# Modulation pieces of layer 1 moved from the end of layer 0's experts into the heads of a DeltaNet layer

## The chip, the cores and the metric

The kernel runs on one core of a Trainium2 chip. The metric is the device time of one execution in microseconds (us): the median of three runs is 1553.63 us (1552.72 to 1554.36).

## The reference, cut to what matters

One inference step of a two-layer backbone over 128 context tokens and 512 latent tokens of 1024 features (five tiles of 128 tokens). Layer 0 is attention beside a convolution module, layer 1 a bidirectional gated DeltaNet with 8 heads; each layer ends in a mixture of 16 experts. Both layers are modulated by rows that come from a conditioning vector (one for the context, one for the latents):

```python
def modulation(cond, w, b):
    return (jax.nn.silu(cond) @ w + b)[:, None, :]      # w: 1024 x 6144, per layer

for layer in range(DEPTH):
    mod_p = jnp.split(modulation(c_ctx[None], w_mod[layer], b_mod[layer]), MOD_CHUNKS, -1)
    mod_s = jnp.split(modulation(c, w_mod[layer], b_mod[layer]), MOD_CHUNKS, -1)
    hp = modulate(rms_norm(xp, g_norm1[layer]), mod_p[0], mod_p[1])
    hs = modulate(rms_norm(xs, g_norm1[layer]), mod_s[0], mod_s[1])
    ...                                                  # attention (0) or DeltaNet (1)
    xp = xp + mod_p[2] * mp
    xs = xs + mod_s[2] * ms
    xp = xp + mod_p[5] * hier_moe(modulate(rms_norm(xp, g_norm2[layer]), mod_p[3], mod_p[4]), *mo)
    xs = xs + mod_s[5] * hier_moe(modulate(rms_norm(xs, g_norm2[layer]), mod_s[3], mod_s[4]), *mo)
```

The change concerns the last five of the twelve column blocks (512 columns each) of layer 1's modulation. Their rows are first used after the eight heads of the DeltaNet layer, in the gate of its output and in its experts.

## The kernel before, in words

Every engine runs its own hand-written list of instructions; semaphores order them across engines, and nothing is scheduled by a planner. The stages in order are layer 0's projections and attention, its output and routing, its experts (about 424 to 624 us), a norm and the gates of layer 1 (to 660 us), the eight heads (to 1198 us), the output, and layer 1's experts to the end.

**Modulation steps.** A step is half a column block: sixteen products of a 128x2 stationary operand (the two conditioning vectors) with 128x128 pieces of the weights (`block_rows`, line 343; a product shows as two matrix instructions in the trace). There are 40 steps; 30 lie beside earlier work. The last ten (`late_load`, `late_steps`) lie at the end of layer 0's experts: SyncE (SP) loads ten pieces of 1 MB each (line 329) into buffers that the experts have given up, and TensorE (PE) does the products after the last expert tile, five steps before it reports the end of its stage and five after. ScalarE (ACT) copies the sums out of PSUM at the start of the next stage (`comb0_act`, line 1965).

**The end of the experts.** Fourteen tiles of 128 routed tokens are gathered, multiplied and scattered back into `ysum` with an accumulating indirect DMA that GpSimd (POOL) issues (line 1724). A scatter waits for the one before it. After the fourteen tiles comes a loop of at least one extra tile, with its own loads (lines 1651, 1652, 1655), gather and scatter. Layer 1's experts (to the end of the kernel) are the same code with other weights and no modulation steps. When all four engines have reported the end (`comb_sp`), SP loads `ysum` (line 1957) and the norm of layer 1 begins; PE does some products that nobody reads in between (line 1463, `unread_products`).

**A head.** PE builds the inverse of a triangular matrix in `levels` (5120 small 32x32 products over the heads, line 2345), alternating with VectorE (DVE) and `fill` pieces of the next head's projection (line 2283); then it runs a scan of five steps (`keys_on_state` 2415, `solve` 2421, `queries_on_state` 2427, `values` 2432 and 2434), again alternating with DVE (residuals 2701, outputs 2729 and 2731) and ACT, with `fill` pieces in the gaps. In the last step:

```python
values(h, 3)
fill(3)
keys_on_state(h, 4)
fill(3)
solve(h, 4)
fill(3)
queries_on_state(h, 4)
values(h, 4)
fill(5)                      # then levels(h + 1) waits for outputs(h, 4) of DVE
```

SP's list for head h (`heads_sp`) is: decay rows of the next head (line 2069), wait for the last values of the head before, two state loads of 64 KB (2084), the weights of head h+2 in three loads of 512 KB (2064; for the last two heads instead one 2 MB load, 2090), and the stores of two final states (2093). POOL adds the bias to the modulation rows, stores them and loads the gate rows (`finish_rows`, `load_gate_rows`) at the start of its part of the heads (`heads_pool`), ahead of its masks for head 0 (2822 to 2825).

Of the kernel before, what the change touches and what calls it, by code (L numbers as in the profile page):

```python
# [22 lines left out]
P = 128  # L23
# [94 lines left out]
def build_program(nc, I, O):  # L118
    with ExitStack() as ctx:
        def sb(name, shape, dt=F32):  # L120
# [13 lines left out]
                 "cb_y0": ("mod_w0", 16), "cb_y1": ("mod_w1", 16), "cb_y2": ("mod_w2", 16), "cb_y3": ("mod_w3", 16), "cb_y4": ("mod_vec", 64),  # L134
                 "hd_kT": ("mod_vecT", 4), "hd_tkn": ("mod_col_mm", 4), "hd_kk": ("mod_step_mm", 40),
                 "hd_cp": ("mod_vec_ev", 4), "hd_silu": ("cond_ready", 1), "hd_rk": ("in_hT_act", 10), "hd_knT": ("mod_raw", 6),
# [4 lines left out]
                 "hd_rows": ("in0_w_lat", 16), "hd_states": ("in0_w_glu", 32), "mod_late_w0": ("mod_step_w0", 240), "mod_late_w1": ("mod_step_w1", 240)}  # L141

# [17 lines left out]
        ring = sb("ring", [P, 3, 4096])  # L160
# [53 lines left out]
        phase_no = {}  # L214
# [38 lines left out]
        def load_act(act):  # L253
# [19 lines left out]

        late_slot = [ring[:, 1, 0:2048], ring[:, 1, 2048:4096], hbuf_flat[:, 0:2048], at(8192, 2048), at(10240, 2048),
                     ring[:, 2, 2048:4096], modN_flat[:, 0:2048], hT_flat[:, 0:2048], hT_flat[:, 2048:4096], modN_flat[:, 2048:4096]]
        LATE_FIRST = 5
        LATE_FREE = [("gu", 12), ("gu", 12), ("x", 24), ("gu", 13), ("gu", 13), ("dn", 24), ("dn", 26), ("gu", 14), ("gu", 14), ("dn", 28)]

        def step_slot(i):
            if i >= MSTEP_LATE:  # L280
                return late_slot[i - MSTEP_LATE]
            return at(2048 + 2048 * (i % 2), 2048) if i < MSTEP_IN0 else ring[:, 0, 2048 * (i % 2):2048 * (i % 2 + 1)]
# [9 lines left out]
        def step_psum(i):  # L292

            l, b, half = step_block(i)
            n = b - 4
            if b < 4:
                return bank(7, P, b * P)
            if l == 0:
                return bank(7, P, n * P) if n < 4 else bank(3, P, (n - 4) % 4 * P)
            return bank(7, P, n % 3 * P) if n < 3 else bank(7, P, (n - 3) * P) if n < 7 else bank(0, P)  # L300

# [20 lines left out]

        def late_load(sp, i):
            l, b, half = step_block(i)
            j = i - MSTEP_LATE
            what, n = LATE_FREE[j]
            sp.wait_ge(S({"gu": "moe0_gu_mm", "x": "moe0_xT", "dn": "moe0_dn_mm"}[what]), n)
            w = I["w_mod"][l].rearrange("(k p) n -> p k n", p=P)
            sp.dma_start(step_slot(i).rearrange("p (k n) -> p k n", k=4),
                         w[:, 4 * half:4 * half + 4, b * 512:(b + 1) * 512]).then_inc(S(f"mod_late_w{j // LATE_FIRST}"), 16)  # L330

        def late_steps(pe, part):
            count_wait(pe, f"mod_late_w{part}", 16 * LATE_FIRST)
            for i in range(MSTEP_LATE + LATE_FIRST * part, MSTEP_LATE + LATE_FIRST * (part + 1)):
                l, b, half = step_block(i)
                block_rows(pe, step_slot(i), step_psum(i), 4 * half, 4 * half + 4).then_inc(S("mod_step_mm"), 1)

# [1311 lines left out]
        def moe_sp(sp, l):  # L1649
# [55 lines left out]
            with sp.Fori(0, n) as i:  # L1705
# [3 lines left out]
                down_at(e, 0)  # L1709
            if l == 0:  # L1710
                for i in range(MSTEP_LATE, MSTEP):
                    late_load(sp, i)

# [64 lines left out]
        def moe_pe(pe, l):  # L1778
# [77 lines left out]
            with pe.Fori(0, n) as i:  # L1856
# [4 lines left out]
                down(i + NS, 0, part(NS), i * 16 + 80)  # L1861
            if l == 0:
                late_steps(pe, 0)
                arrive(pe, "pe")
                late_steps(pe, 1)
                for other in ("act", "dve", "pool"):
                    pe.wait_ge(S(f"{other}_phase_done"), phase_no["moe0"])
            else:
                barrier(pe, "pe", "moe1")

# [92 lines left out]
        def comb0_act(act):  # L1963
            act.activation(view(small, 1099, 1), C("eps"), ACT.Sqrt)
            raw_out(act, MSTEP, raw_row[:, 3 * P:7 * P], bank(7))
            act.copy(raw_row[:, 7 * P:8 * P], bank(0, P)).then_inc(S("mod_raw"), 1)

            def square(t):
                act.wait_ge(S("cb_used"), t + 1)
                act.activation(junk[:], X[:, t, :], ACT.Square, accum_out=ss[:, t:t + 1])  # L1970
                act.drain()
                act.activation(rstd[:, t:t + 1], ss[:, t:t + 1], ACT.Sqrt, scale=1.0 / D, bias=C("eps")).then_inc(S("norm_rms"), 1)

            for t in range(NT):
# [77 lines left out]
        def heads_sp(sp):  # L2052
# [23 lines left out]
            count_wait(sp, "hd_rows", 16)  # L2076
            decay_rows(0)
            for h in range(H):
                if h + 1 < H:
# [3 lines left out]
                for c, name in ((0, "state_fwd"), (1, "state_bwd")):  # L2083
                    sp.dma_start(St[:, c, :], I[name][0, 0, h]).then_inc(S(f"hd_st{c}"), 16)
                if h + 2 < H:
                    head_weights(h + 2)
# [15 lines left out]
        def gates_pe(pe):  # L2102
# [13 lines left out]
            unread_products(pe, 3)  # L2116
            pe.wait_ge(S("mod_raw"), 6)
            for t in range(NT):
# [152 lines left out]
        def heads_pe(pe):  # L2271
# [172 lines left out]
            for h in range(H):  # L2444
# [24 lines left out]
                values(h, 1)  # L2469
                fill(1)  # L2470
                if more:
                    k_to_tokens(n)
# [16 lines left out]
                fill(1)  # L2489
                queries_on_state(h, 3)  # L2490
                values(h, 3)
                fill(3)
                keys_on_state(h, 4)
                fill(3)
                solve(h, 4)
                fill(3)
                queries_on_state(h, 4)
                values(h, 4)
                fill(5)
            barrier(pe, "pe", "heads1")  # L2500

        def heads_act(act):
# [103 lines left out]
            for h in range(H):  # L2606
# [6 lines left out]
                if more:  # L2613
                    take_unit(n, 0)
                inverse_blocks(h)
                if more:
                    take_unit(n, 1)
# [192 lines left out]
        def heads_pool(pool):  # L2810
            pool.memset(TTp, 0.0)
            pool.drain()
            pool.wait_ge(S("mod_bias"), 320)
            finish_rows(pool, 1, 3, 8)
            pool.wait_ge(S("mod_stored"), 192)
            load_gate_rows(pool, 1, 2, "mod_bc")
            for h in range(H):
# [6 lines left out]
                count_wait(pool, "hd_masked", 2 * h + 1)  # L2824
                pool.tensor_tensor(NTm, A, rep(betam[:, h, :], P, 2), ALU.mult).then_inc(S("hd_masked"), 1)
            barrier(pool, "pool", "heads1")

# [186 lines left out]
```

## Time and profile before

| | |
|---|---|
| median of three runs | 1553.63 us (1552.72 to 1554.36) |
| the profiled execution | 1549.61 us |
| its span, first to last instruction | 1547.5 us |
| mean granted TensorE clock | 0.971 |
| busy share of the span | PE 90%, PE weight load 62%, DVE 53%, ACT 30%, POOL 13% |
| bytes moved by DMA | 265.45 MB, mean 172 GB/s |

The profile is of one execution. A busy share is an average over stages with different limits, so the stages are read one by one: the chain of work that ended last says which engine or transfer set the time of each stretch, and the timelines of the engines say how much another engine had left beside it. In a timeline the columns are the start and the duration of a group of instructions, then the engine, the line, the operation, the tiles written and read, the size and the count; a bracket gives the idle time before the group and what ended it. "issue" there is time in which the engine waited for nothing that the profile shows.

### The profile page before, as it was taken

The page shows a single profiled execution, that of the slowest core. Times are in us where ns is not written, and L with a number is a line of the kernel's source. Part 1 is how long each engine was busy: PE and PEld are TensorE (multiplying, and loading weights), DVE is VectorE, ACT ScalarE, POOL GpSimd, SP SyncE. Part 2 cuts the span into 40 slices and gives each one's busy share as a digit, 9 for nine tenths or more (in the row PEclk, how much of TensorE's full clock was granted, in tenths as well). Part 3 has the DMA queues.
Part 4 walks back from the last instruction along what each step waited for, and adds up shares of the span by engine and source line. Part 5 has one row for each costly group of instructions (what it writes and reads, how often), then busy time and mean ns, then how long its engine had stood idle before and what let it go on. Part 6 is the DMA issues. An engine that isn't in the chain of part 4 may idle for free.

```text
span 1547.5 us, 33618 instructions
## 1 busy us (share of the span) xinstructions
PE 1397.3 (90%) x14422; PEld 964.2 (62%) x14422; DVE 814.2 (53%) x1604; ACT 470.1 (30%) x1057; POOL 205.1 (13%) x199
## 2 busy tenths in 40 slices
PE   4999989999899997779998898998988999899993
PEld 3555557745487776456776776776755445587772
DVE  2377678736633432535666565665653726544331
ACT  3101755512100000544555544554522202100000
POOL 2200020101321212131011010110100001312221
PEclk9999999999999998889999999999999999999997
DMA  9954673222799999521101201111010432899985
GB/s 344 339 168 136 201 236 121 72 109 109 253 369 360 386 368 299 158 90 41 46 22 49 64 23 47 52 37 60 6 61 4 163 127 104 294 367 374 380 288 132
DMA packets 103412, 265.45 MB, mean 172 GB/s; under 512 B 7648, under 2 KB 37608, under 8 KB 93888
## 3 DMA queue, kind: packets, MB, share of 16 engines
q1 hardware_dynamic: 88096, 206.22, 36.7%
q0 software_dynamic: 15168, 57.08, 12.9%
q8 instruction: 114, 1.87, 0.5%
q14 instruction: 34, 0.28, 0.1%
HBM read 235.29 MB, written 35.32 MB: 175 GB/s over the span
## 4 chain that ended last, share of the span: by engine, by line
PE 61%; DMA 13%; DVE 11%; issue 7%; ACT 4%; DVEq 2%; POOL 1%; POOLq 0%; ACTq 0%; SPq 0%
DMA ysum<-arena,small 11%; PE psum L983 8%; PE psum L2283 8%; PE psum L1794 5%; PE psum L635 5%; PE psum L2345 4%; PE psum L1805 3%; PE psum L2295 2%; PE psum L2842 2%; PE psum L343 2%; PE psum L533 2%; PE psum L999 2%; PE psum L1010 1%; PE psum L1022 1%; DVE modN L2655 1%
## 5 line engine op out<-in xcount | busy, mean ns | idle before, releaser
L2283 PE MATMUL psum<-hT,ring 128*128 128x384 f32 (+1 forms) x736 | 242.9, 455 | 0.7 <-ACTq L218 0.7
L2283 PEld LDWEIGHTS psum<-hT,ring 128*128 128x128 f32 x736 | 129.1, 195 | 35.4 <-issue 3.9
L1794 PEld LDWEIGHTS psum<-arena,ring 128*128 128x128 f32 x1024 | 119.0, 196 | 12.3 <-issue 10.3
L1794 PE MATMUL psum<-arena,ring 128*128 128x128 f32 x1024 | 120.5, 280 | 4.1 <-DVE arena L1873 4.1
L1915 DVE TENSOR_TENSOR arena<-arena,psum 128x256 f32<-128x256 f32 x30 | 12.6, 421 | 191.0 <-PE psum L1794 166.5
L792 DVE SCALAR_TENSOR_TENSOR arena<-arena,params_sb 128x655 f32<-128x655 f32 x120 | 106.1, 906 | 6.3 <-issue 0.9
L2345 PEld LDWEIGHTS psum<-arena 32*32 32x32 f32 x5120 | 54.7, 109 | 65.7 <-issue 38.0
L1724 POOL DMA_INDIRECT ysum<-arena,small x34 | 57.6, 1693 | 263.4 <-DMA ysum<-arena,small 138.2
L2345 PE MATMUL psum<-arena 32*32 32x32 f32 x5120 | 63.6, 198 | 30.4 <-issue 18.7
L983 PE MATMUL psum<-ring,arena 128*128 128x512 f32 x160 | 72.6, 608 | 1.0 <-ACTq L218 1.0
L635 PE MATMUL psum<-hT,ring 128*128 128x512 f32 (+1 forms) x256 | 72.1, 438 | 0.7 <-ACT modN L463 0.7
L1894 ACT ACTIVATE arena<-psum 128x256 f32<-128x256 f32 x30 | 11.5, 384 | 200.6 <-PE psum L1794 173.0
L983 PE MATMUL psum<-ring,hT 128*128 128x512 f32 x160 | 70.7, 596 | 1.2 <-ACTq L218 1.2
L1873 ACT COPY arena<-psum 128x512 f32<-128x512 f32 x30 | 17.6, 586 | 167.0 <-PE psum L1786 167.0
L2822 POOL TENSOR_TENSOR arena<-arena,consts_sb 128x640 f32<-128x640 f32 x8 | 10.5, 1317 | 383.7 <-PE psum L2395 383.4
L1805 PE MATMUL psum<-ring,arena 128*128 128x512 f32 x128 | 57.8, 594 | 1.3 <-DVE arena L1915 1.3
L635 PEld LDWEIGHTS psum<-hT,ring 128*128 128x128 f32 x256 | 38.3, 191 | 30.8 <-issue 30.8
L983 PEld LDWEIGHTS psum<-ring,arena 128*128 128x128 f32 x160 | 30.1, 194 | 36.5 <-issue 34.7
L983 PEld LDWEIGHTS psum<-ring,hT 128*128 128x128 f32 x160 | 29.7, 190 | 36.1 <-issue 34.6
L1305 DVE TENSOR_TENSOR arena<-psum,modG 128x512 f32<-128x512 f32 x20 | 13.8, 689 | 69.7 <-PE psum L983 69.7
L1881 DVE SCALAR_TENSOR_TENSOR arena<-psum,small,junk 128x512 f32<-128x512 f32 x60 | 42.8, 748 | 11.0 <-PE psum L1805 7.0
L1794 PEld LDWEIGHTS psum<-arena 128*128 128x128 f32 x384 | 43.8, 192 | 2.9 <-issue 2.9
(517 smaller groups left out, 2753.5 us busy)
## 6 DMA issues: line engine op xcount, KB each, us to landing
arena<-in_w_mod SPq DMA_DIRECT2D x18, 1024.0 KB, 5.3
ring<-in_m_w_gate SPq DMA_DIRECT2D x18, 1024.0 KB, 7.3
ring<-in_m_w_up SPq DMA_DIRECT2D x18, 1024.0 KB, 9.5
ring<-in_m_w_down SPq DMA_DIRECT2D x18, 1024.0 KB, 10.9
ring<-in_w_mod SPq DMA_DIRECT2D x17, 1024.0 KB, 5.5
modN<-in_m_w_down SPq DMA_DIRECT2D x16, 1024.0 KB, 13.4
ring<-in_c_w_in SPq DMA_DIRECT2D x24, 512.0 KB, 6.4
arena<-in_m_w_gate SPq DMA_DIRECT2D x8, 1024.0 KB, 8.4
```

The costliest lines, as they stand in the source:

```text
L343: m = pe.matmul(out[32 * j:32 * j + 2, :], cond[:, k, :], w[:, c0:c0 + P], start=(k == 0), stop=(k == KC - 1))
L533: m = pe.matmul(bank(t, LAT), hT[:, k, tok(t)], ring[:, 0, k * LAT:(k + 1) * LAT], start=(k == 0), stop=(k == KC - 1))
L635: m = pe.matmul(out, ring[:, s, c0:c0 + P], hT[:, k, o:o + n], start=(k == 0), stop=(k == KC - 1))
L792: m = dve.scalar_tensor_tensor(out=acc[:, fc, :], in0=src, scalar=conv_w(fc, k), in1=acc[:, fc, :], op0=ALU.mult, op1=ALU.add)
L983: m = pe.matmul(out_bank(l, n), lhs[:, k, tok(t)], ring[:, OUT_SLOT[l][nb], k * 512:(k + 1) * 512], start=(k == 0), stop=(k == KC - 1))
L999: m = pe.matmul(bank(b, n0), qT[0:QK, h, tok(qt)], kT[0:QK, h, k0 * P:k0 * P + n0], start=True, stop=True)
L1724: pool.indirect_dma_start(out=ysum[l], out_offset=bass.IndirectOffsetOnAxis(ap=idx, axis=0), in_=yb[q][part, :], in_offset=None, compute_o ...
L1794: m = pe.matmul(bank((2, 4)[half] + (1, 3)[half] * q, P, f * P), gu_slot[s][:, c0:c0 + P], xgT[:, q, k, :], start=(k == 0), stop=(k == KC ...
L1805: m = pe.matmul(bank(5 + nb), hidT[:, q, k, :], dn_slot[s][:, k * D + nb * 512:k * D + nb * 512 + 512], start=(k == 0), stop=(k == 1))
L1881: dve.scalar_tensor_tensor(out=yb[q][:, c], in0=bank(5 + half), scalar=w, in1=gate_row[:, c], op0=ALU.mult, op1=ALU.mult).then_inc(S(f"moe ...
L2283: m = pe.matmul(bank(un % 2, w), ring[:, s, c0k:c0k + P], hT[:, k, o:o + w], start=(k == 0), stop=(k == KC - 1))
L2345: m = pe.matmul(bank(b, 32, 32 * i)[QD(q), :], lhs(5 * g + i, q), rhs(5 * g + i, q), start=True, stop=True)
```

## The change

The ten late steps leave the end of layer 0's experts. Each of the first five heads now takes one column block: SP loads its 2 MB in five pieces into free parts of `ring` and `arena`, and PE does its 32 products in four places of the head's last scan step, eight products (sixteen matrix instructions) a place. For head 0 the load follows the first decay rows; for heads 1 to 4 it stands between the state loads and the loads of weights, behind a wait for the last late products of the head before. PE waits for the load and for DVE's transition before the first place. ACT copies the sums out in the next head, between the inverse blocks and a projection copy, and PE waits for that copy ahead of `k_to_tokens`. POOL's finishing of the rows moves from before its masks of head 0 to after those of head 7. The semaphore counts that follow from this are adjusted.

```diff
-        late_slot = [ring[:, 1, 0:2048], ring[:, 1, 2048:4096], hbuf_flat[:, 0:2048], at(8192, 2048), at(10240, 2048),
-                     ring[:, 2, 2048:4096], modN_flat[:, 0:2048], hT_flat[:, 0:2048], hT_flat[:, 2048:4096], modN_flat[:, 2048:4096]]
+        LATE_HEADS = (MSTEP - MSTEP_LATE) // 2
+        late_slot = [ring[:, 0, 3072:4096], ring[:, 1, 3072:4096], at(15360, 1024), ring[:, 2, 640:1152], ring[:, 2, 3200:3712]]
+        late_row = lambda k: late_slot[k // 2][:, k % 2 * 512:k % 2 * 512 + 512] if k < 6 else late_slot[k - 3]
+        LATE_K = [(0, 2), (2, 4), (4, 6), (6, 8)]
...
-        def late_load(sp, i):
...
+        def late_load(sp, h):
+            if h >= 1:
+                count_wait(sp, "late_mm", h)
+            l, b, _ = step_block(MSTEP_LATE + 2 * h)
             w = I["w_mod"][l].rearrange("(k p) n -> p k n", p=P)
+            k = 0
+            for slot in late_slot:
+                n = slot.shape[1] // 512
+                sp.dma_start(slot.rearrange("p (k n) -> p k n", k=n), w[:, k:k + n, b * 512:(b + 1) * 512]).then_inc(S("late_w"), 16)
+                k += n
+
+        def late_rows(pe, h, part):
+            if part == 0:
+                count_wait(pe, "late_w", 16 * len(late_slot) * (h + 1))
+                count_wait(pe, "hd_nt", h + 2)
+            for k in range(*LATE_K[part]):
+                m = block_rows(pe, late_row(k), bank(3, P, 2 * P), k, k + 1)
+            if part == len(LATE_K) - 1:
+                m.then_inc(S("late_mm"), 1)
...
# moe_sp
-            if l == 0:
-                for i in range(MSTEP_LATE, MSTEP):
-                    late_load(sp, i)
# moe_pe
-            if l == 0:
-                late_steps(pe, 0)
-                arrive(pe, "pe")
-                late_steps(pe, 1)
-                for other in ("act", "dve", "pool"):
-                    pe.wait_ge(S(f"{other}_phase_done"), phase_no["moe0"])
-            else:
-                barrier(pe, "pe", "moe1")
+            barrier(pe, "pe", f"moe{l}")
# comb0_act
-            raw_out(act, MSTEP, raw_row[:, 3 * P:7 * P], bank(7))
-            act.copy(raw_row[:, 7 * P:8 * P], bank(0, P)).then_inc(S("mod_raw"), 1)
# heads_sp
             decay_rows(0)
+            late_load(sp, 0)
...
                     sp.dma_start(St[:, c, :], I[name][0, 0, h]).then_inc(S(f"hd_st{c}"), 16)
+                if 1 <= h < LATE_HEADS:
+                    late_load(sp, h)
                 if h + 2 < H:
                     head_weights(h + 2)
# gates_pe
-            pe.wait_ge(S("mod_raw"), 6)
# heads_pe
                 values(h, 1)
                 fill(1)
+                if 1 <= h <= LATE_HEADS:
+                    count_wait(pe, "late_raw", h)
                 if more:
                     k_to_tokens(n)
...
+                late = (lambda part: late_rows(pe, h, part)) if h < LATE_HEADS else (lambda part: None)
                 values(h, 3)
                 fill(3)
+                late(0)
                 keys_on_state(h, 4)
                 fill(3)
+                late(1)
                 solve(h, 4)
                 fill(3)
+                late(2)
                 queries_on_state(h, 4)
                 values(h, 4)
                 fill(5)
+                late(3)
# heads_act
                 inverse_blocks(h)
+                if 1 <= h <= LATE_HEADS:
+                    count_wait(act, "late_mm", h)
+                    act.copy(raw_row[:, (2 + h) * P:(3 + h) * P], bank(3, P, 2 * P)).then_inc(S("late_raw"), 1)
# heads_pool
-            pool.wait_ge(S("mod_bias"), 320)
-            finish_rows(pool, 1, 3, 8)
-            pool.wait_ge(S("mod_stored"), 192)
-            load_gate_rows(pool, 1, 2, "mod_bc")
             for h in range(H):
...
+            pool.wait_ge(S("mod_bias"), 320)
+            count_wait(pool, "late_raw", LATE_HEADS)
+            finish_rows(pool, 1, 3, 8)
+            pool.wait_ge(S("mod_stored"), 192)
+            load_gate_rows(pool, 1, 2, "mod_bc")
             barrier(pool, "pool", "heads1")
```

## Rows read from the trace of the kernel before

**Rows 1.** Chain of waits, end of layer 0's experts: start us, us, what.

```profile
562.77 8.91 DMA ysum<-arena,small
...
591.94 8.72 DMA ysum<-arena,small
...
603.17 8.95 issue
```

**Rows 2.** Chain of waits, end of layer 1's experts.

```profile
1487.31 8.01 DMA ysum<-arena,small
...
1510.14 6.25 DMA ysum<-arena,small
...
1518.91 6.75 issue
```

**Rows 3.** Stretches of both expert ends: us, engines busy, PE clock, DMA share, GB/s.

```profile
562.77:623.25 60.48, 48.16 (x531) 39.17 (x530) 16.12 (x26) 2.33 (x5) 12.90 (x11) 0.91 0.94 302
1487.31:1535.50 48.19, 35.40 (x235) 27.88 (x233) 15.40 (x26) 2.33 (x5) 12.15 (x11) 0.95 0.64 152
```

**Rows 4.** Timeline of SP's queue, the last of seven groups of late loads.

```profile
593.72 5.19 SPq L329 DMA_DIRECT2D modN<-in_w_mod  x1
```

**Rows 5.** Timeline of PE, the last late products at the end of layer 0's experts.

```profile
623.34 1.65 PE L343 MATMUL psum<-modN,small 128*2 128x128 f32 x25 [3.62 <-issue]
```

**Rows 6.** Chain of waits, start of the kernel: late-type products with nothing between.

```profile
37.18 1.86 PE psum L343 x64
```

**Rows 7.** Timeline of PE, last scan step of head 0; last row: start of head 4.

```profile
746.23 2.10 PE L2283 MATMUL psum<-hT,ring 128*128 128x384 f32 x6
748.17 0.61 PE L2415 MATMUL psum<-ring,arena 128*128 128x128 f32 x4
...
753.18 2.32 PE L2283 MATMUL psum<-hT,ring 128*128 128x256 f32 x10
756.70 0.91 PE L2345 MATMUL psum<-arena 32*32 32x32 f32 x80 [1.20 <-DVE arena L2731]
...
939.17 0.91 PE L2345 MATMUL psum<-arena 32*32 32x32 f32 x80 [1.54 <-DVE arena L2731]
```

**Rows 8.** Timeline of DVE, the residuals of head 0's last scan step.

```profile
748.59 0.61 DVE L2701 SCALAR_TENSOR_TENSOR ring<-psum,small,arena 128x128 f32<-128x128 f32 x2 [1.81 <-PE psum L2415]
```

**Rows 9.** Timeline of SP's queue: weights at head 1's start, 2 MB at head 6's.

```profile
755.53 2.31 SPq L2064 DMA_DIRECT2D ring<-in_c_w_in  x3
...
1062.25 0.38 SPq L2090 DMA_DIRECT2D ring<-in_c_w_in  x1
```

**Rows 10.** Timeline of PE, first long wait in the levels of heads 1 and 6.

```profile
763.33 0.45 PE L2345 MATMUL psum<-arena 32*32 32x32 f32 x32 [1.35 <-issue]
...
1070.06 0.53 PE L2345 MATMUL psum<-arena 32*32 32x32 f32 x21 [3.27 <-issue]
```

**Rows 11.** DMA queues: instruction queue, whole span, then 1067.4 to 1070.1 us: packets, MB, share.

```profile
q8 instruction: 114, 1.87, 0.5%
...
q8 instruction: 1, 0.02, 2.5%
```

**Rows 12.** Stretches of the levels of heads 1, 2, 3, 4 and 6.

```profile
756.70:780.44 23.74, 21.20 (x792) 15.48 (x792) 13.29 (x38) 13.77 (x28) 0.00 (x0) 1.00 0.28 70
817.11:840.38 23.27, 21.15 (x791) 15.38 (x791) 13.41 (x38) 13.43 (x28) 0.00 (x0) 1.00 0.29 72
877.07:902.14 25.07, 22.31 (x791) 16.53 (x791) 13.28 (x38) 13.59 (x28) 0.00 (x0) 0.93 0.27 66
939.17:965.36 26.19, 22.40 (x792) 16.66 (x792) 13.41 (x38) 13.20 (x28) 0.00 (x0) 0.93 0.24 62
...
1063.76:1090.99 27.23, 22.53 (x791) 15.94 (x791) 13.62 (x39) 13.35 (x28) 0.00 (x0) 0.94 0.23 79
```

**Rows 13.** Timeline of DVE, a convolution beside POOL's finishing and one without it.

```profile
663.23 2.95 DVE L2658 SCALAR_TENSOR_TENSOR modN<-modN,params_sb 128x641 f32<-128x641 f32 x2
...
1097.76 1.85 DVE L2658 SCALAR_TENSOR_TENSOR modN<-modN,params_sb 128x641 f32<-128x641 f32 x2
```

More of the change, by code:

```diff
@@ L134, in build_program @@
                  "cb_y0": ("mod_w0", 16), "cb_y1": ("mod_w1", 16), "cb_y2": ("mod_w2", 16), "cb_y3": ("mod_w3", 16), "cb_y4": ("mod_vec", 64),
-                 "hd_kT": ("mod_vecT", 4), "hd_tkn": ("mod_col_mm", 4), "hd_kk": ("mod_step_mm", 40),
-                 "hd_cp": ("mod_vec_ev", 4), "hd_silu": ("cond_ready", 1), "hd_rk": ("in_hT_act", 10), "hd_knT": ("mod_raw", 6),
+                 "hd_kT": ("mod_vecT", 4), "hd_tkn": ("mod_col_mm", 4), "hd_kk": ("mod_step_mm", 30),
+                 "hd_cp": ("mod_vec_ev", 4), "hd_silu": ("cond_ready", 1), "hd_rk": ("in_hT_act", 10), "hd_knT": ("mod_raw", 4),
                  "hd_conv": ("mod_col", 3), "hd_kn": ("in_hT_dve", 10),
@@ L140, in build_program @@
                  "lgw_shift": ("in0_latT", 3), "last_hT": ("in0_latT_ev", 3), "last_rstd": ("in0_sq", 11), "last_base": ("outputs", 32),
-                 "hd_rows": ("in0_w_lat", 16), "hd_states": ("in0_w_glu", 32), "mod_late_w0": ("mod_step_w0", 240), "mod_late_w1": ("mod_step_w1", 240)}
+                 "hd_rows": ("in0_w_lat", 16), "hd_states": ("in0_w_glu", 32), "late_w": ("mod_step_w0", 240), "late_mm": ("ln_tok", 5), "late_raw": ("at_o", 5)}
         def S(name):
@@ L272, in build_program @@
         first_slot = [ring[:, 1, :], at(12288, 4096), ring[:, 2, :], at(8192, 4096)]
-        late_slot = [ring[:, 1, 0:2048], ring[:, 1, 2048:4096], hbuf_flat[:, 0:2048], at(8192, 2048), at(10240, 2048),
-                     ring[:, 2, 2048:4096], modN_flat[:, 0:2048], hT_flat[:, 0:2048], hT_flat[:, 2048:4096], modN_flat[:, 2048:4096]]
-        LATE_FIRST = 5
-        LATE_FREE = [("gu", 12), ("gu", 12), ("x", 24), ("gu", 13), ("gu", 13), ("dn", 24), ("dn", 26), ("gu", 14), ("gu", 14), ("dn", 28)]
+        LATE_HEADS = (MSTEP - MSTEP_LATE) // 2
+        late_slot = [ring[:, 0, 3072:4096], ring[:, 1, 3072:4096], at(15360, 1024), ring[:, 2, 640:1152], ring[:, 2, 3200:3712]]
+        late_row = lambda k: late_slot[k // 2][:, k % 2 * 512:k % 2 * 512 + 512] if k < 6 else late_slot[k - 3]
+        LATE_K = [(0, 2), (2, 4), (4, 6), (6, 8)]
         def step_slot(i):
-            if i >= MSTEP_LATE:
-                return late_slot[i - MSTEP_LATE]
             return at(2048 + 2048 * (i % 2), 2048) if i < MSTEP_IN0 else ring[:, 0, 2048 * (i % 2):2048 * (i % 2 + 1)]
@@ L299, in step_psum @@
                 return bank(7, P, n * P) if n < 4 else bank(3, P, (n - 4) % 4 * P)
-            return bank(7, P, n % 3 * P) if n < 3 else bank(7, P, (n - 3) * P) if n < 7 else bank(0, P)
+            return bank(7, P, n % 3 * P)
         def mod_sp(sp):
@@ L321, in step_load @@
                          w[:, 4 * half:4 * half + 4, b * 512:(b + 1) * 512]).then_inc(S(f"mod_step_w{i % 2}"), 16)
-        def late_load(sp, i):
[L324 to L327, printed above, removed]
-            w = I["w_mod"][l].rearrange("(k p) n -> p k n", p=P)
[L329 to L336, printed above, removed]
+        def late_load(sp, h):
+            if h >= 1:
+                count_wait(sp, "late_mm", h)
+            l, b, _ = step_block(MSTEP_LATE + 2 * h)
+            w = I["w_mod"][l].rearrange("(k p) n -> p k n", p=P)
+            k = 0
[11 more added lines that the diff above has]
+                m.then_inc(S("late_mm"), 1)
         def block_rows(pe, w, out, k0, k1):
```

## The prediction

> **What bounds the kernel now.** I read the chain of waits first, because PE's 90% busy share is an average and says nothing of a single stage. At the end of layer 0's experts the chain is not on PE: from 562.77 us on it runs through one accumulating scatter after another, 8.91 us, 8.72 us and so on, and then through 8.95 us in which POOL waits for the extra tile [rows 1]. The same code ends layer 1, and there the scatters take 8.01 us and then 6.25 us, and the wait 6.75 us [rows 2]. The view of stretches sets the two ends side by side, from the scatter of the tenth tile to the last landing: 60.48 us with DMA at 302 GB/s in layer 0, 48.19 us at 152 GB/s in layer 1 [rows 3]. What layer 0 has in addition is the ten late loads, of which SP issues the last at 593.72 us [rows 4]. The late products are not on this chain: their last group on PE starts at 623.34 us, with POOL's last landing already in, and nothing after it waits for them [rows 5]. So the experts' end is set by transfers, and the late steps lengthen it through their loads alone.
>
> In the heads, PE and DVE hand the chain to each other. I read PE's timeline of a last scan step: PE goes through `fill` and the state products without a pause, and only at the start of the next levels does it wait, 1.20 us in heads 0 to 2 (1.54 us in heads 3 and 4), for DVE's last outputs [rows 7]. DVE in turn waited 1.81 us for the keys product behind the `fill` [rows 8].
>
> **The change, part by part.** The sum is made against the profiled execution, 1549.61 us (span 1547.5); the median of the three runs lies 4.0 us above it, and I add the sum to the median.
>
> *The experts' end.* With the late loads gone, layer 0's end should take what layer 1's takes, as both run the same list: 48.19 - 60.48 = **-12.3 us** [rows 3]. At the bad end, only the scatters issued after the last late load gain, about 4 us: 8.72 - 6.25 = 2.5 for a scatter and 8.95 - 6.75 = 2.2 for the wait, less some. I take -12.3, since nothing else distinguishes the two ends. The products that leave cost nothing where they were (hidden by the scatters), and ACT's two copies out were hidden by the loads of `ysum`. PE now idles for about ten us ahead of the unread products and may start them at the lower clock; they would take up to twice their time beside DVE's additions, so I set 0, at most +1.
>
> *The products in the heads.* 64 matrix instructions take 1.86 us back to back [rows 6], so a place of sixteen costs 0.465 us and a head 1.86 us. The first place stands ahead of `keys_on_state`, for which DVE waits [rows 8], so its 0.465 us moves the whole DVE chain. The other three lie under it until PE's 1.20 us are used up: PE arrives at the next levels 1.86 - 1.20 = 0.66 us later than DVE did before. A head so costs the larger, 0.66 us in heads 0 to 2 and 0.465 us in heads 3 and 4 (their idle is 1.54 [rows 7]): **+2.9 us**. The ends are 5 x 0.465 = 2.3 and, if nothing hides, 5 x 1.86 = 9.3. Behind PE's new waits stand the state products, but the loads are asked for some 50 us earlier, and DVE's transition is done before the place is reached. ACT's copy out falls in a gap ahead of the new values, and PE's wait for it comes some 8 us later: 0 each.
>
> *The loads in the heads.* This is the term on which all hangs. The 2 MB of heads 1 to 4 are issued when the head before ends, that is at the start of the densest stretch of PE's list, with the 1.5 MB of weights, issued today at 755.53 us [rows 9], queued behind on SP. Nobody needs either of them soon. But PE waits there already: 1.35 us in the levels of head 1, for nothing that the profile shows, and 3.27 us in those of head 6 [rows 10], which begin just after a single 2 MB load [rows 9]. In that wait one packet of 16 KB moves on the queue for instructions (114 packets carry 1.87 MB in all), in the stretch just before PE resumes [rows 11]. I read this as PE running out of instructions while the next piece of its list queues behind data. The levels tell its price: 23.74, 23.27, 25.07 and 26.19 us in heads 1 to 4 with weights alone, together 98.27, and 27.23 us in head 6, though its 2 MB came alone [rows 12]. After a long wait the granted clock falls too (0.94 in head 6, 1.00 in heads 1 and 2 [rows 12]). For the four heads I take 26.71, halfway between the worst head with weights (26.19) and head 6 (27.23), as both kinds of load now follow each other: 4 x 26.71 - 98.27 = **+8.6 us**. The ends are 0 (the wait is of another making) and, with a second long wait of 3.27 us in each head beside the longer traffic, 4 x 30.5 - 98.27 = +23.7. Head 0's load lies beside the gates, where PE's list is sparse and the decay rows are ahead of it on the queue: 0, at most +1.
>
> The Trainium skill, "Runtime: NRT & Kernel Launch", section "Instruction fetch mechanics", says that the sequencer fetches the next 16 KiB of its list by a DMA queue of its own while it runs the present one, and that crossing a boundary is mostly hidden. By that rule this term would be about 0; the 3.27 us of head 6 speak against it [rows 10], and no row before shows the longer traffic itself.
>
> *POOL's finishing.* Beside it the two taps of head 0's first convolution took 2.95 us, against 1.85 us elsewhere [rows 13]. Moved behind the masks of head 7 it falls on that very convolution of head 7: -1.1 and +1.1, so 0, with -1 and +1 as ends. Its DMAs end some 80 us before the heads do.
>
> Sum: -12.3 + 2.9 + 8.6 = **-0.8 us**, so 1548.8 us for the profiled execution and 1552.8 us beside the median. A difference under 0.2% (3.1 us) can't be told from none.
>
> **The rivals.** *The loads cost nothing in the heads.* For it speaks that heads 1 and 2 lose only some 1.4 us in that wait with 1.5 MB under way; against it, that the two heads with a 2 MB load, 6 and 7, both waited over 3 us. Then -12.3 + 2.9 + 1 = -8.4, **1545.2 us**. This is also where the skill's rule leads.
>
> *Two long waits a head: slower.* The traffic at a head's start lasts about twice as long as today, 3.5 instead of 1.5 MB, and PE asks for the next piece of its list again before it is over. At 23.7 us for the four heads the sum is +14.3, **1567.9 us**. It decides from 12.5 us on (12.3 - 2.9 + 3.1), that is 3.1 us a head. Against it: in head 6 the second piece came without such a wait.
>
> *The experts' end hardly gets shorter.* The first scatters of the two stretches differ little, 8.91 and 8.01 us [rows 1, 2], so it may be the scatters themselves, and layer 0's tokens. At -4 the sum is -4 + 2.9 + 8.6 = +7.5, **1561.1 us**. Against it: in layer 1, once the weights have landed, the same scatters come down to 6.25 us [rows 2].
>
> **How the numbers follow.** My forecast has 0.55, and its own range is 1548 to 1558; of that 0.11 is faster by over 0.2%, 0.38 within, 0.06 slower. The rival without cost in the heads has 0.25 (0.24 faster, 0.01 within), the two long waits 0.12 and the unchanged end 0.08, both slower. That gives 0.35, 0.39 and 0.26. The range from 1544.5 to 1561 takes in the first rival and most of the third, and leaves the second out.
>
> **What would show it.** Right: the stretch from the tenth tile's scatter to the last landing in layer 0 takes 47 to 50 us; the levels of heads 1 to 4 take 26 to 28 us each, with an "issue" wait of about 3 us in them and the granted clock under 1; PE's wait for DVE ahead of the levels of heads 1 to 5 is nearly gone; head 7's first convolution is slower and head 0's faster. Wrong: levels of 23 to 24 us (the first rival), two waits over 2.5 us in a head (the second), or scatters of 8 to 9 us at the end of layer 0 with no load beside them (the third).

## The result: slower by 0.8%

The kernel after takes 1566.52 us (median of 7 runs, 1558.08 to 1570.5), the one before beside it 1550.88 us (7 runs, 1546.17 to 1554.36): a ratio of 1.0082, with a 95% interval from 1.0055 to 1.0109 (some 12.7 us; the quotient of the two medians alone is 1.0101). Ratios here and below are of fast runs; one slow run, of the experiment e5 at 1729.83 us with a granted clock of 0.803, is left out. The profiled executions are 1566.52 us (span 1564.4) and 1549.61 us (span 1547.5), 16.9 us apart. They can be laid against each other by the start of the first product of each head's `levels` and the start of the last group but one in them (line 2395 before, 2387 after); `scan` is what lies from there to the next head's levels.

| stretch, us | before | after | difference | predicted |
|---|---|---|---|---|
| start to head 0's levels | 693.92 | 682.66 | -11.3 | -12.3 |
| levels of heads 1 to 4 | 98.27 | 115.79 | +17.5 | +8.6 |
| levels of heads 0, 5, 6, 7 | 107.41 | 109.34 | +1.9 | 0 |
| scan parts of heads 0 to 4 | 184.11 | 191.04 | +6.9 | +2.9 |
| scan parts of heads 5 and 6 | 73.85 | 74.97 | +1.1 | 0 |
| the rest | 389.96 | 390.57 | +0.6 | 0 |

**The experts' end** got shorter as foreseen. In the chain of waits of the kernel after (start us, us, what) the scatters at that place are down to layer 1's 6.25 us, and so is POOL's wait for the extra tile; before, they took 8.72 and 8.95 us [rows 1, 2]:

```profile
588.00 6.22 DMA ysum<-arena,small
...
596.75 6.57 issue
...
613.62 3.70 DMA arena<-ysum
```

The stretch from the scatter that stood at 562.77 us before [rows 1] (563.92 us now) to the last landing takes 49.2 us, inside the 47 to 50 that were to show it right. The start of head 0's levels differs by a few us between executions, but over the twelve traces of this study it lies at 678.3 to 682.7 us in the seven kernels without late loads at the experts' end and at 688.6 to 693.9 us in the five with them.

**The levels** lost more than that. These are the stretches of the levels of heads 1 to 4 in the kernel after, with the columns of [rows 12]:

```profile
747.64:776.38 28.74, 23.73 (x796) 16.94 (x792) 13.41 (x38) 14.05 (x28) 0.00 (x0) 0.82 0.45 131
814.59:845.95 31.36, 27.12 (x795) 18.30 (x791) 13.73 (x38) 15.43 (x29) 0.00 (x0) 0.78 0.42 121
884.16:911.61 27.45, 23.89 (x796) 17.45 (x792) 13.41 (x38) 14.37 (x28) 0.00 (x0) 0.88 0.47 137
949.81:978.06 28.25, 23.91 (x796) 16.87 (x792) 13.52 (x38) 14.41 (x28) 0.00 (x0) 0.88 0.45 133
```

Two columns tell the story. DMA's share rose from 0.24 to 0.29 [rows 12] to 0.42 to 0.47, and the granted clock fell from 0.93 to 1.00 to 0.78 to 0.88. PE's busy time in these four stretches is 98.65 us, against 87.06 us before for the same products, so +11.6 us are the same work at the lower clock; the time in which PE is not busy grew from 11.21 to 17.15 us, +5.9. The timeline of PE in the kernel after shows that idle time as waits for nothing that the profile shows ("issue"), in most cases in the middle of a group of like products, in heads 1 to 4:

```profile
753.80 0.45 PE L2337 MATMUL psum<-arena 32*32 32x32 f32 x32 [0.87 <-issue]
...
761.18 1.02 PE L2323 MATMUL psum<-consts_sb,junk 128*128 128x1 f32 x5 [4.13 <-issue]
...
819.25 0.22 PE L2337 MATMUL psum<-arena 32*32 32x32 f32 x2 [1.43 <-issue]
829.87 0.42 PE L2337 MATMUL psum<-arena 32*32 32x32 f32 x12 [1.50 <-issue]
839.70 0.25 PE L2337 MATMUL psum<-arena 32*32 32x32 f32 x4 [1.23 <-issue]
...
893.07 0.31 PE L2337 MATMUL psum<-arena 32*32 32x32 f32 x11 [3.46 <-issue]
...
961.64 0.44 PE L2337 MATMUL psum<-arena 32*32 32x32 f32 x27 [3.40 <-issue]
```

How a wait and the clock hang together is seen around the 4.13 us of head 1, in three stretches of the kernel after (columns as above):

```profile
747.64:757.00 9.36, 8.49 (x347) 6.47 (x344) 5.65 (x14) 9.23 (x16) 0.00 (x0) 1.00 0.92 291
757.00:761.20 4.20, 0.07 (x2) 0.09 (x2) 0.38 (x2) 0.97 (x2) 0.00 (x0) 0.64 0.96 231
761.20:768.50 7.30, 7.30 (x171) 4.72 (x171) 2.34 (x7) 0.00 (x0) 0.00 (x0) 0.51 0.03 7
```

While the loads fill the DMA engines (0.92, then 0.96) PE works and then stands still. When they are done (0.03) PE goes on, without a pause (7.30 us busy of 7.30), but at a granted clock of 0.51, the lower of its two levels, 1.2 instead of 2.4 GHz.

**The scan parts.** The chain of waits of the kernel after, in the last scan step of head 0, shows what a place of sixteen matrix instructions costs:

```profile
738.94 1.94 PE psum L2275 x6
740.88 0.55 PE psum L346 x16
741.43 0.64 PE psum L2413 x4
...
743.92 0.64 PE psum L2419 x4
744.56 0.45 PE psum L2424 x4
```

The place takes 0.55 us, not 0.465, and the four state products behind it take 0.64 us, where such products without a place ahead of them take 0.45 (line 2424). Three places at 0.75 and a last one at 0.55 are 2.8 us; less the idle time of 1.20 or 1.54 us that PE had [rows 7] that is 1.6 or 1.3 us a head, and 1.52 or 1.18 us were measured (38.21 us against 36.69 and 37.03).

**POOL's finishing** now stands beside a convolution of head 7, which takes what head 0's took before [rows 13]. The timeline of DVE in the kernel after:

```profile
1112.79 2.96 DVE L2660 SCALAR_TENSOR_TENSOR modN<-modN,params_sb 128x641 f32<-128x641 f32 x2
```

### The profile page after: what moved, and what is told of

Same layout as the page of the kernel before. It is cut to its first block, busy times and chain, and to the rows that moved or that the text cites. A ratio compares the mean times of both kernels' runs of the same rounds, so it can differ in the third digit from the quotient of the medians.

```text
span 1564.4 us, 33641 instructions
## 1 busy us (share of the span) xinstructions
PE 1414.9 (90%) x14422; PEld 967.9 (62%) x14422; DVE 814.9 (52%) x1604; ACT 470.7 (30%) x1060; POOL 204.0 (13%) x199
## 4 chain that ended last, share of the span: by engine, by line
PE 70%; DVE 8%; DMA 8%; issue 7%; ACT 4%; DVEq 1%; POOL 1%; POOLq 0%; ACTq 0%; SPq 0%
PE psum L2275 10%; PE psum L986 8%; PE psum L1794 8%; DMA ysum<-arena,small 6%; PE psum L638 5%; PE psum L2337 4%; PE psum L1805 4%; PE psum L346 3%; PE psum L2287 2%; PE psum L2845 2%; PE psum L536 2%; PE psum L1002 2%; PE psum L1013 1%; PE psum L1814 1%; PE psum L1025 1%
## 5 line engine op out<-in xcount | busy, mean ns | idle before, releaser
L2275 PE MATMUL psum<-hT,ring 128*128 128x384 f32 (+1 forms) x736 | 250.6, 466 | 0.7 <-ACTq L218 0.7
L2820 POOL TENSOR_TENSOR arena<-arena,consts_sb 128x640 f32<-128x640 f32 x8 | 10.5, 1318 | 420.6 <-PE psum L2387 409.5
L1466 PE MATMUL psum<-consts_sb 128*128 128x512 f32 x90 | 46.9, 679 | 10.6 <-POOLq L218 10.6
L2761 DVE TENSOR_TENSOR arena<-psum,consts_sb 128x160 f32<-128x160 f32 x64 | 20.8, 325 | 56.3 <-PE psum L2337 55.0
```

Of the source, the lines that this page charges most:

```text
L1466: pe.matmul(bank(4), ident, consts[:, 0:512], start=True, stop=True)
L2275: m = pe.matmul(bank(un % 2, w), ring[:, s, c0k:c0k + P], hT[:, k, o:o + w], start=(k == 0), stop=(k == KC - 1))
```

## The experiments

Theory L was that the loads at a head's start hold up PE's instruction fetch in the levels; rival P that the products, by lengthening PE's list and by their effect on its clock, do it, and the loads only run beside. The table has every kernel's levels of heads 1 to 4, split into PE busy and PE not busy, from the view of stretches; the diffs and expectations follow it. A row's levels are those of one execution, while the times are of all: the executions of one kernel spread over 7 to 20 us, so a few us between two rows show little by themselves.

| kernel | levels 1 to 4, us | busy | not busy | DMA share | time against before [95%] |
|---|---|---|---|---|---|
| before | 98.3 | 87.1 | 11.2 | 0.24 to 0.29 | 1 |
| after | 115.8 | 98.7 | 17.2 | 0.42 to 0.47 | 1.0082 [1.0055, 1.0109] |
| e1_loads_in_scan | 102.5 | 89.8 | 12.7 | 0.25 to 0.28 | 1.0010 [0.9988, 1.0033] |
| e2_no_loads | 104.1 | 91.0 | 13.1 | 0.23 to 0.29 | - |
| e3_few_products | 113.9 | 94.3 | 19.5 | 0.44 to 0.46 | - |
| e5_before_loads | 106.2 | 91.2 | 15.0 | 0.40 to 0.46 | 1.0074 [1.0051, 1.0097] |
| e6_all_in_scan | 92.7 | 87.9 | 4.9 | 0.02 | 0.9833 [0.9803, 0.9863] |
| e7_before_weights_in_scan | 87.8 | 83.6 | 4.2 | 0.02 | 0.9831 [0.9798, 0.9863] |
| e4_one_place | 97.2 | 85.8 | 11.4 | 0.25 to 0.27 | 0.9982 [0.9956, 1.0008] |
| e8_before_shifted | 110.1 | 96.5 | 13.7 | 0.23 to 0.26 | 1.0030 [1.0003, 1.0058] |
| e9_scan_one_place | 87.9 | 84.1 | 3.8 | 0.02 | 0.9848 [0.9811, 0.9886] |
| e10_late_loads_alone | 98.7 | 90.4 | 8.2 | 0.20 to 0.22 | 0.9928 [0.9904, 0.9951] |

**e1_loads_in_scan**, the kernel after with

```diff
-            late_load(sp, 0)
-                if 1 <= h < LATE_HEADS:
-                    late_load(sp, h)
+                if h < LATE_HEADS:
+                    count_wait(sp, "hd_sv", 10 * h + 2)
+                    late_load(sp, h)
                 for c, name in ((2, "new_sf"), (3, "new_sb")):
```

> The late loads of a head leave SP only when values of the head's scan step 0 are made (hd_sv, 10h+2), some 4 us into the scan, so the levels run without them; the products stay where they are. Theory L (the loads hold up PE's instruction fetch in the levels): the levels of heads 1 to 4 fall from 115.8 us in sum to 98 to 101, the scan parts of heads 0 to 4 stay at 38.2 or grow by up to 1 us a head, and the time is the time before -11 (experts' end) +7 (products) +0 to +6, i.e. 0.997 to 1.002 of before. Rival P (the products alter PE's instruction list and its clock, the loads only run beside it): the levels stay at 112 to 116 and the time stays near 1.008 of before.

Levels of 102.5 us and scan parts of 38.21 us, at 1.001 of before: theory L's side. The transfer is the same, only later, and some 11 us of the loss are gone (1.0082 against 1.0010). But the levels did not come back to 98.3. The stretches of heads 1 and 2 in e1, with the weights as the only large load:

```profile
743.34:767.88 24.54, 22.14 (x795) 15.90 (x791) 13.40 (x38) 14.04 (x28) 0.00 (x0) 0.93 0.28 68
806.09:832.39 26.30, 22.57 (x795) 15.90 (x791) 13.63 (x38) 14.31 (x28) 0.00 (x0) 0.94 0.26 64
```

**e2_no_loads**, the kernel after without its calls of `late_load` and without PE's wait for `late_w`.

> The late loads are left out altogether and the products read whatever lies in the slots. Theory L: levels of heads 1 to 4 at 98 to 100 us in sum, time 0.996 to 0.999 of before; it should be the fastest of the variants that keep the products in four places. Rival P: levels at 112 to 116, time near 1.008.

Levels of 104.1 us: neither theory's. Without the loads PE still waits longer than before (13.1 against 11.2 us). That points at something that stays in this kernel, though in one execution of each so small a difference doesn't show it. The whole time of this kernel (1681.49 us) and of the next (1588.36 us) says nothing, since with other modulation values layer 1 routes its tokens otherwise and runs another number of products; only their heads are read.

**e3_few_products**, the kernel after with

```diff
-            for k in range(*LATE_K[part]):
-                m = block_rows(pe, late_row(k), bank(3, P, 2 * P), k, k + 1)
             if part == len(LATE_K) - 1:
+                for j in range(4):
+                    m = pe.matmul(bank(3, P, 2 * P)[32 * j:32 * j + 2, :], cond[:, 7, :], late_row(7)[:, j * P:j * P + P], start=True, stop=True)
```

> The late loads stay at the head's start; of the 32 products of each late block only four are made, after fill(5) at the head's end, so layer 1's last modulation blocks lack the rest. Theory L: the levels of heads 1 to 4 stay at 112 to 116 us in sum; the scan parts of heads 0 to 4 fall from 38.2 to 36.7 to 37.1, some 6 us in all; time 1.003 to 1.005 of before. Rival P: levels back to 98 to 101, time 0.993 to 0.996 of before.

Levels of 113.9 us with 28 of 32 products gone, and scan parts of 36.67 and 37.02 us in heads 1 to 4, as before the change. (Head 0's took 39.87 us; there the granted clock stayed at 0.50 from 705 us to the end of its levels and beyond.) So the products cost what the scan parts show, and the long levels need the loads.

**e5_before_loads**, the kernel before with an `extra_load` that is `late_load` without a consumer:

```diff
             decay_rows(0)
+            extra_load(sp, 0)
...
+                if 1 <= h < LATE_HEADS:
+                    extra_load(sp, h)
                 if h + 2 < H:
                     head_weights(h + 2)
```

> The kernel before, with the same 2 MB loaded into the same slots at the start of each of heads 0 to 4 and nothing reading them: experts' end, products and finishing are those of before. Theory L: the levels of heads 1 to 4 grow from 98.3 to 112 to 118 us in sum and the time is 1.009 to 1.013 of before. Rival P: the levels stay at 98 to 100 and the time is that of before within 0.2%.

1.0074 of before by the loads alone, below the 1.009 to 1.013 that theory L had asked for (the interval reaches 1.0097), and far from rival P's 1. In the profiled execution, the fastest of the seven that count, the levels of heads 1 to 4 grew by 7.9 us, not by 17.5. In the whole times the loads cost the same with and without the products: 0.74% here, 0.72% between e1 and the kernel after, some 11 us each. Heads 1 and 4 of this kernel:

```profile
753.85:780.07 26.22, 22.66 (x792) 16.76 (x792) 13.29 (x38) 14.04 (x28) 0.00 (x0) 0.93 0.44 134
...
941.54:970.40 28.86, 24.76 (x791) 18.37 (x791) 13.40 (x38) 12.97 (x28) 0.00 (x0) 0.82 0.40 119
```

Theory L in its first form doesn't explain what e1 and e2 have over the kernel before. What they and the kernel after share is another list: a product takes two matrix instructions and two weight loads, so a block's 32 products add 128 of PE's instructions to each of heads 0 to 4, and the ten steps that left took 640 away ahead of the heads. If the list is fetched in pieces of 256 (PE's 28844 matrix instructions and weight loads come in 114 packets [rows 11], 253 a packet), the pieces end where they ended before in heads 1 and 3, and 128 instructions away in heads 2 and 4. The next four kernels look at the loads (any of them, the weights too) and at that position one by one.

**e6_all_in_scan** is e1 with the weights behind the late loads, **e7_before_weights_in_scan** the kernel before with the weights moved and nothing else (the 2 MB loads of the last two heads stand behind the same wait):

```diff
                 for c, name in ((0, "state_fwd"), (1, "state_bwd")):
                     sp.dma_start(St[:, c, :], I[name][0, 0, h]).then_inc(S(f"hd_st{c}"), 16)
+                count_wait(sp, "hd_sv", 10 * h + 2)
                 if h + 2 < H:
                     head_weights(h + 2)
```

> Late loads as in e1_loads_in_scan, and the head's own weight loads (1.5 MB for the head after next) go behind them, also after values of scan step 0, so that only the states and the decay rows are loaded at a head's start. Theory L (any load of SP beside the levels holds up PE's instruction fetch): levels of heads 1 to 4 fall from e1's 102.5 us in sum to 92 to 97, those of heads 0, 5, 6 by 1 to 3 each as well, and the time is 0.988 to 0.996 of before. Rival Q (the waits that are left come from where the 256-instruction pieces of PE's list end inside the levels, whatever is loaded): levels of heads 1 to 4 at 100 to 105, time 0.999 to 1.003.

> The kernel before with the head's weight loads issued after values of scan step 0; nothing else is changed. Theory L: levels of heads 1 to 4 fall from 98.3 us to 91 to 95 in sum, and with heads 0, 5, 6 the time is 0.992 to 0.997 of before. Rival Q: levels at 97 to 100, the time that of before within 0.2%.

Both went further than theory L had it: 0.9833 and 0.9831. One wait on SP takes some 25 us off the kernel before (26 us by the ratio; 24 us between the medians, 1548.84 and 1524.68). The stretches of heads 1 to 4 in e7:

```profile
750.10:771.63 21.53, 20.89 (x791) 15.32 (x791) 13.29 (x38) 13.75 (x28) 0.00 (x0) 1.00 0.02 5
808.30:830.22 21.92, 20.91 (x791) 15.26 (x791) 13.41 (x38) 13.70 (x28) 0.00 (x0) 1.00 0.02 5
866.90:888.75 21.85, 20.96 (x792) 15.32 (x792) 13.41 (x38) 13.38 (x28) 0.00 (x0) 1.00 0.02 5
925.76:948.27 22.51, 20.85 (x792) 15.32 (x792) 13.41 (x38) 12.98 (x28) 0.00 (x0) 1.00 0.02 4
```

With nothing large beside them the levels take 22 us at the full clock. So the 98.3 us of the kernel before held 10.5 us of the same loss already, by its weights (not busy 11.2 to 4.2, busy 87.1 to 83.6). The waits do not vanish, but in the timeline of PE in e7 the longest of these heads is that of head 4:

```profile
939.41 0.26 PE L2346 MATMUL psum<-arena 32*32 32x32 f32 x8 [1.25 <-issue]
```

One head of e6, head 2, lost its clock without any large load beside it; its stretch, and its longest wait in the timeline of PE:

```profile
801.16:828.31 27.15, 24.84 (x796) 17.80 (x792) 13.95 (x39) 15.44 (x29) 0.00 (x0) 0.85 0.02 5
```

```profile
820.04 0.32 PE L2337 MATMUL psum<-arena 32*32 32x32 f32 x4 [1.37 <-issue]
```

Its clock was at 0.85 over the stretch, and it took 27.15 us, where heads 1, 3 and 4 of that kernel took 21.5 to 22.6.

**e4_one_place** is e1 with all 32 products after the last `fill`:

```diff
-        LATE_K = [(0, 2), (2, 4), (4, 6), (6, 8)]
+        LATE_K = [(0, 0), (0, 0), (0, 0), (0, 8)]
```

> As e1_loads_in_scan, but all 32 products of a late block stand in one place, after fill(5) at the head's end. If a place costs its 16 matrix instructions (0.55 us) and a slower product behind it (0.2 us more), four places in one save three of the slower ones: the scan parts of heads 0 to 4 fall from 38.2 us to 37.4 to 37.8 and the time by 2 to 4 us against e1. If the cost is the products alone, the scan parts stay at 38.1 to 38.3 and the time is e1's.

The scan parts fell to 37.28 us, a little under the range, and the time to 0.9982, 0.28% under e1 (4.3 us; the two intervals overlap). In the chain of waits of this kernel the 64 matrix instructions cost what they cost at the kernel's start [rows 6], and `levels` behind them starts as ever:

```profile
740.97 1.86 PE psum L346 x64
742.83 0.68 PE psum L2337 x50
```

**e8_before_shifted**, the kernel before with

```diff
+            for _ in range(32):
+                pe.matmul(bank(4, 2)[0:2, :], consts[:, 0:2], consts[:, 0:2], start=True, stop=True)
             unread_products(pe, 3)
```

> The kernel before with 32 unread products (two columns by two) ahead of the gates' rows, so that every later 256-instruction piece of PE's list ends 128 instructions sooner inside the levels; loads and heads are those of before. The products themselves take about 2 us once. Rival Q (position sets the waits): the levels of heads 1 to 4 differ from 98.3 us in sum by more than 3, with the single waits moved and of other lengths. Theory L alone: they stay at 97 to 100 and the time is that of before, +0 to +2 us.

Levels of 110.1 us, 11.9 more than before, with loads and heads untouched: rival Q's finding. But the profiled execution is the slowest of ten (1564.63 us, with a median of 1555.15), and in it the levels of the other four heads were 3.9 us shorter. The whole time is 1.0030 of before, and of these 4.6 us the products themselves take 1.6. Head 1, 23.74 us before [rows 12], is the longest:

```profile
753.90:783.89 29.99, 24.92 (x791) 17.72 (x791) 13.94 (x39) 14.72 (x29) 0.00 (x0) 0.84 0.23 56
```

```profile
760.47 0.31 PE L2347 MATMUL psum<-arena 32*32 32x32 f32 x12 [3.45 <-issue]
776.57 0.32 PE L2347 MATMUL psum<-arena 32*32 32x32 f32 x15 [1.62 <-issue]
```

Its waits are longer than the 1.35 us of [rows 10], and they stand where the shift puts them. The view of stretches counts PE's instructions from the start of head 1's levels to the wait, first in the kernel before, then in e8, there to the second wait too:

```profile
756.70:761.97 5.27, 5.27 (x216) 3.46 (x216) 3.17 (x9) 5.17 (x14) 0.00 (x0) 1.00 1.10 277
...
753.90:757.01 3.11, 3.10 (x152) 2.15 (x152) 2.12 (x5) 3.07 (x7) 0.00 (x0) 1.00 1.05 270
753.90:774.93 21.03, 17.58 (x663) 12.26 (x664) 9.87 (x26) 10.03 (x19) 0.00 (x0) 0.92 0.32 78
```

Before, 432 matrix instructions and weight loads come ahead of the wait; in e8 it is 304, just 128 fewer, and the second wait comes 1023 later, four pieces of 256 but for one. PE resumes 6.6 us after the start of the levels in both: the wait is longer because it begins sooner. Counted in this way, all 65 gaps over 0.6 us that PE has in the levels of heads 1 to 4 in the traces of the twelve kernels stand within three instructions of where the kernel before has its first wait in that head, shifted by what each kernel's list adds or lacks, or a whole number of 256 from there. Each ends 1.2 to 1.7 us after a packet of 16 KB has landed on the instruction queue.

The shift has either sign. In e1, e2, e4 and e8, with the weights alone beside them and the pieces' ends 128 instructions away, head 2 took 25.25 to 29.24 us against 23.27 before, and head 4 took 24.05 to 24.85 against 26.19. So both were right in part: traffic makes the waits long, and where the pieces of the list end decides how long, and which groups they hit. Without traffic the position costs little (not busy 4.9 us in e6, 4.2 us in e7, whose lists differ by these 128 instructions a head).

**e9_scan_one_place** joins e6 and e4.

> e6_all_in_scan with the 32 products of a late block in one place, as in e4_one_place. If the two savings add up, the scan parts of heads 0 to 4 fall from 38.2 to 37.3 us as they did in e4, the levels of heads 1 to 4 stay at 88 to 93 us in sum, and the time is 4 to 6 us under e6's: 0.978 to 0.981 of before. If the levels lose again what the scan gains (the products at the head's end bring PE's list closer to the levels), levels grow by some 5 us and the time stays at 0.983.

Scan parts of 37.28 us and levels of 87.9 us, as hoped, and the profiled execution is the shortest of this study, 1513.69 us. But its six runs spread from 1513.69 to 1533.41 us with a median of 1524.0, a ratio of 0.9848: no better than e6 or e7 as far as these intervals tell. Only one run has a trace, so where the others lost the 4.7 us of the scan parts again stays open.

**e10_late_loads_alone** is e5 with the weights moved as in e7.

> e5_before_loads (late blocks loaded at the head's start, nothing reads them) with the head's own weights moved into the scan as in e7, so that 2 MB in pieces of 2 KB are the only large load beside the levels. Levels of heads 1 to 4 were 87.8 us in sum with neither load, 98.3 with the weights alone, 106.2 with both. If a load costs by its bytes wherever it stands, they come to 95 to 103 and the time to 0.988 to 0.994 of before. If only the small pieces of the weights (512 B) hold up the instruction fetch, or if the two loads cost only together, they stay at 87 to 91 and the time at 0.983.

98.65 us and 0.9928, inside what loads that cost by their bytes would give. Heads 1 and 3:

```profile
752.89:776.89 24.00, 22.09 (x791) 16.42 (x792) 13.30 (x38) 13.32 (x28) 0.00 (x0) 0.93 0.22 82
...
874.61:901.46 26.85, 25.14 (x791) 18.19 (x792) 13.31 (x38) 13.65 (x28) 0.00 (x0) 0.81 0.20 73
```

The four corners nearly add up: neither load 87.8 us, weights 98.3, late blocks 98.7, both 106.2, so 10.5 and 10.9 us alone and 18.4 us together, one execution each. Two megabytes in large pieces cost the levels as much as 1.5 MB in small ones.

## Why the prediction was wrong

The sum was -0.8 us; the ratio makes it some +12.7, and the profiled executions differ by +16.9. Step by step, in the profiled executions:

- **The experts' end (-12.3): right.** -11.3 us up to head 0's levels; the scatters with no load beside them took layer 1's time. (In the chain of waits of the kernel after, PE's expert products stand ahead of the last tile's scatter, up to 584 us, where the chain ran through scatters before.)
- **The products in the heads (+2.9): mis-sized, +6.9.** The step that failed is "a place of sixteen costs 0.465 us", taken from 64 in a row [rows 6]. In four places it is 0.55 us, and 0.20 us more in the products that follow. The rest of the step held: with all products in one place (e4) the scan parts grew by 0.59 to 0.61 us in heads 0 to 2 and by 0.25 and 0.23 us in heads 3 and 4, about the 0.66 and 0.32 us that the idle time leaves of 1.86.
- **The loads in the heads (+8.6): the mechanism was right, the size was not, +17.5.** The step that failed is "for the four heads I take 26.71, halfway between the worst head with weights and head 6". The four took 27.45 to 31.36 us. Two things were mis-sized or missing. The clock stood in the prediction only as a remark on head 6 (0.94), while in the kernel after it was 0.78 to 0.88 and cost 11.6 us of busy time, twice the 5.9 us that the added waits cost. And the prediction took the waits of before as a property of each head; e8 shows that they move when PE's list is shifted by 128 instructions, and the change shifts it so in heads 2 and 4. How the +17.5 divides between loads and list, single executions don't settle (+7.9 with the loads alone in e5, +4.2 with the new list alone in e1). By the whole times the loads cost some 11 us with the products or without them. What is left for the list is an estimate from e1, whose ratio is 1.5 us over before where the other rows of the table give -2.7: some 4 us, give or take 3.5.
- **The range:** the products and the loads came out inside their own ends (2.3 to 9.3, and 0 to 23.7), but the range from 1544.5 to 1561 had no room for both high at once.
- **The rival "two long waits a head"** was nearest in time (1567.9 us, with a chance of 0.12), and the levels did pass its 12.5 us. But no head had two waits over 2.5 us, as it wanted: heads 1, 3 and 4 had one each (4.13, 3.46 and 3.40), and head 2 three of 1.2 to 1.5. Two thirds of the levels' loss (11.6 of 17.5 us) were busy time at the lower clock.
- **The rival "the loads cost nothing"** falls with e5: the same bytes, read by nobody, cost 0.74%. So does the rule of the Trainium skill beside it ("Runtime: NRT & Kernel Launch", section "Instruction fetch mechanics": crossing into the next 16 KiB is mostly hidden). With the queues quiet the trace nearly agrees: PE is not busy for 4.2 us in four heads (e7). With loads under way it does not: 17.2 us in the kernel after.
- **Head 0's load (0):** its levels grew by 0.7 us, inside the bound of 1. **POOL's finishing (0):** the loss at head 7 was seen, +1.1 us in the scan parts of heads 5 and 6; a gain at head 0 can't be told apart inside the -11.3.

The prediction read the wait for nothing shown as PE's instruction fetch, from one packet on the instruction queue [rows 11]. The traces bear the reading out: the waits stand at the ends of pieces of 256 instructions in all twelve kernels, each ends 1.2 to 1.7 us after a packet of 16 KB has landed, and they grow with the loads beside them. No run changed the fetch itself, and what holds a packet back beside other traffic stays open; the packets themselves took 0.9 to 2.0 us in the kernel after, little other than the 0.9 to 1.6 in e7.

## What to carry to other kernels

Before a load is moved to "a quiet time", look at what PE's instruction list does at that time, not only at who needs the data: large loads beside hundreds of short matrix instructions cost PE waits, and a wait can cost the clock after it as well. Compare variants by the whole times of many executions: the levels of one execution of e5 and of e8 said 7.9 and 11.9 us, where the ratios say some 11 and 5 for the whole kernel. Here the same loads, issued some 30 us later beside the longer products of the scan, cost no time that can be seen there, and moving the old weight loads alone gave 1.7%. Price small products put between others with the change to and from them: four places of sixteen cost 2.8 us, one place of 64 cost 1.86.

## What the runs showed of the hardware that was not expected

- The levels of heads 1 to 4 in which DMA's share is 0.02 take some 22 us, at 0.2 to 0.3 from 23 to 30, at 0.4 to 0.47 from 25 to 31, with the same products; the one exception without traffic is e6's head 2 with 27.15.
- The waits in PE's list of short products come at steps of 256 instructions, one packet of 16 KB, and moving the list by 128 instructions moved them by 128 (e8). With the weights alone beside them, head 2's levels were slower by it and head 4's faster in each of e1, e2, e4 and e8.
- The granted clock fell during a wait of 4.13 us and was 0.51 for the next 7.3 us, in which PE was busy throughout; in e6 a wait of 1.37 us in a head without traffic went with 0.85 over the stretch. Not every wait did it. Of the 48 stretches of heads 1 to 4 in the twelve traces, the nine without a wait over 0.9 us all kept 1.00; of the other 39, 28 fell below it and eleven kept it, among them e4's head 2 with a wait of 2.71 us (its stretch, then the wait). What decides between them stays open.

```profile
804.47:829.72 25.25, 21.11 (x796) 15.34 (x792) 13.12 (x37) 13.00 (x27) 0.00 (x0) 1.00 0.25 64
```

```profile
810.41 0.22 PE L2337 MATMUL psum<-arena 32*32 32x32 f32 x2 [2.71 <-issue]
```

- Thirty-two products of two columns, 1.6 us of work some 66 us ahead of the first levels, moved every later wait in the levels of heads 1 to 4, only by moving PE's list. In the slowest of that kernel's ten executions these levels took 11.9 us more; the whole time grew by 0.3%.
